# Gate layer norm moved to GpSimd, gated scaling to ScalarE, earlier reciprocals and two banks for the turned gate tiles

## The reference

```python
o_mla = mla_mixer(h_q, h_kv, k_pe, cos, sin, ...)   # 8 heads, full softmax over 512 keys
# spatial gating branch
z = gelu(h_sg); u, v = z[..., :512], z[..., 512:]
v = layernorm(v, ln_g, ln_b)                        # over the 512 channels of each token
mixed = einsum('hij,bcjhd->bcihd', w_s, v) + b_s    # inside chunks of 128 tokens
o_sg = u * mixed
o = concat([rmsnorm(o_mla, g1), rmsnorm(o_sg, g2)]) # then x = x + o @ w_out
```

## Time and profile before

| | us |
|---|---|
| median of 3 runs | 1542.7 (1542.68 to 1542.95) |
| profiled execution | 1543.31, its span 1541.5 |
| PE busy | 1464.7 (95% of the span) |
| DVE busy | 774.7 (50%) |
| ACT busy | 686.9 (45%) |
| POOL busy | 660.2 (43%) |

### The profile page before, as it was taken

The page is one execution under the profiler, slowest core; times in us unless marked ns, Lnnn a source line. Parts: engine busy times, 40 slices in busy tenths (PEclk is TensorE's granted clock), DMA queues, the critical chain, the costliest instruction groups (busy, mean ns, idle before and its releaser), DMA issues.

```text
span 1541.5 us, 19395 instructions
## 1 busy us (share of the span) xinstructions
PE 1464.7 (95%) x6838; PEld 1194.5 (77%) x6838; DVE 774.7 (50%) x1188; ACT 686.9 (45%) x1084; POOL 660.2 (43%) x317
## 2 busy tenths in 40 slices
PE   4998889999999999999999898999999999999994
PEld 4776669888878888888878565898888888888883
DVE  5738768633454530345164876792526445024443
ACT  4566636444343431344355664563534444124441
POOL 4443226743344444343545321585343444434440
PEclk9999999999999999999999999999999999999997
DMA  5320114521233243322423101354122332323221
GB/s 171 121 84 15 41 55 137 178 82 42 82 96 98 81 122 96 93 82 86 126 83 107 44 28 55 96 175 127 38 86 68 110 101 80 119 82 109 84 67 55
DMA packets 39032, 138.74 MB, mean 90 GB/s; under 512 B 4848, under 2 KB 5104, under 8 KB 38704
## 3 DMA queue, kind: packets, MB, share of 16 engines
q1 hardware_dynamic: 37440, 134.23, 28.4%
q10 hardware_dynamic: 1520, 3.52, 0.7%
HBM read 135.64 MB, written 2.10 MB: 89 GB/s over the span
## 4 chain that ended last, share of the span: by engine, by line
PE 78%; issue 10%; DVE 7%; POOL 4%; ACT 1%; POOLq 0%; DVEq 0%; ACTq 0%
PE ps L1284 25%; PE ps L1286 25%; PE ps L1285 25%; POOL w_lo L340 4%; PE ps L1436 1%; DVE small L988 1%; DVE h_lo L1014 1%; PE ps L1294 1%; DVE work L1091 0%; DVE small L1018 0%; DVE arena L1014 0%; PE ps L1459 0%; DVE work L1000 0%; DVE work L1074 0%; DVE arena L1164 0%
## 5 line engine op out<-in xcount | busy, mean ns | idle before, releaser
L340 POOL TENSOR_TENSOR w_lo<-raw,w_hi 128x1024 fp32r<-128x1024 f32 x248 | 605.0, 2457 | 721.0 <-ACT w_hi L436 720.8
L1284 PE MATMUL ps<-h_hi,w_hi 128*128 128x512 f32 (+1 forms) x1040 | 407.9, 392 | 26.0 <-POOL w_lo L340 20.5
L1285 PE MATMUL ps<-h_lo,w_hi 128*128 128x512 f32 (+1 forms) x1040 | 403.9, 388 | 0.0
L1286 PE MATMUL ps<-h_hi,w_lo 128*128 128x512 f32 (+1 forms) x1040 | 403.9, 388 | 0.0
L436 ACT ACTIVATE w_hi<-raw 128x1024 fp32r<-128x1024 f32 x248 | 255.8, 1054 | 326.6 <-PE ps L1286 326.5
L1284 PEld LDWEIGHTS ps<-h_hi,w_hi 128*128 128x128 f32 x1040 | 195.9, 188 | 69.3 <-issue 28.8
L1284 PE MATMUL ps<-arena,w_hi 128*128 128x512 f32 (+2 forms) x656 | 244.1, 372 | 0.9 <-DVE arena L970 0.9
L1286 PE MATMUL ps<-arena,w_lo 128*128 128x512 f32 (+2 forms) x656 | 241.9, 369 | 0.0
L1285 PE MATMUL ps<-arena,w_hi 128*128 128x512 f32 (+2 forms) x656 | 241.8, 369 | 0.0
L1285 PEld LDWEIGHTS ps<-h_lo,w_hi 128*128 128x128 f32 x1040 | 195.9, 188 | 40.8 <-issue 1.0
L1286 PEld LDWEIGHTS ps<-h_hi,w_lo 128*128 128x128 f32 x1040 | 195.8, 188 | 40.2
(11 more groups left out here) (169 smaller groups left out, 1793.5 us busy)
## 6 DMA issues: line engine op xcount, KB each, us to landing
raw<-blocks_d SPq DMA_DIRECT2D x248, 512.0 KB, 3.5
x<-xT_d SPq DMA_DIRECT2D x4, 512.0 KB, 7.7
work<-memT_d ACTq DMA_DIRECT2D x2, 1024.0 KB, 4.9
outT_d<-work SPq DMA_DIRECT2D x8, 256.0 KB, 2.2
work<-ln_d ACTq DMA_DIRECT2D x2, 512.0 KB, 3.6
par<-par_d ACTq DMA_DIRECT2D x2, 113.5 KB, 2.8
work<-pos_d ACTq DMA_DIRECT2D x1, 128.0 KB, 6.4
mix_g<-par_d ACTq DMA_DIRECT2D x2, 4.0 KB, 6.3
```

The source lines that it names most:

```text
L340: gp.tensor_tensor(w_lo[:, b % SPLIT, :], raw[:, b % RAW, :], w_hi[:, b % SPLIT, :].bitcast(F32), ALU.subtract).then_inc(lo_done.sem, 1)
L1284: pe.matmul(out, a_hi, b_hi, start=first, stop=False)
L1285: pe.matmul(out, a_hi, b_lo, start=False, stop=False)
L1286: return pe.matmul(out, a_lo, b_hi, start=False, stop=last)
```

## The change

- `recip_sums(h)` on DVE moves from the end of step (h, 3) to the end of (h, 2). All four exponentials of the head are then issued already, since ACT runs two steps ahead.
- The layer norm of the gate leaves DVE. DVE computes the roots at (1,1) and signals `gate_root`; POOL runs the three instructions per tile, tiles 0 and 1 at h 1, 2 and 3 at h 2, waiting for its own last instruction inside a tile. The `gate_low` calls follow them. ACT's hi parts move by one step each: SPLIT_STEPS from (1,2), (2,0), (2,2), (3,2) to (2,0), (2,1), (2,3), (3,1).
- The scaling of `u` leaves DVE for ACT, at the same steps, waiting for the new signal `gated_root`.
- `turn_gated(f)` uses banks 4 and 2 by turns, so that f 1 waits for nothing of its kind and f waits for the lo part of f-2. The output projection, whose first bank is 4, now waits for the lo part of f 2.

```diff
-NORM_STEPS = ((1, 1), (1, 3), (2, 1), (3, 1))
-SPLIT_STEPS = ((1, 2), (2, 0), (2, 2), (3, 2))
+ROOT_STEP = (1, 1)
+SPLIT_STEPS = ((2, 0), (2, 1), (2, 3), (3, 1))
...
+        BT = (4, 2)
...
+                def gate_norm(g):
+
+                    if g == 0:
+                        need(gate_root, 1)
+                        need(ln_in, 16)
+                    gp.tensor_scalar(vt[:, g, :], vt[:, g, :], mv[:, g, 0:1], sm_t[:, g:g + 1],
+                                     ALU.subtract, ALU.mult).then_inc(gate_step.sem, 1)
+                    need(gate_step, 2 * g + 1)
+                    gp.tensor_tensor(vt[:, g, :], vt[:, g, :], ln_gb[:, 0, :], ALU.mult).then_inc(gate_step.sem, 1)
+                    need(gate_step, 2 * g + 2)
+                    gp.tensor_tensor(vt[:, g, :], vt[:, g, :], ln_gb[:, 1, :], ALU.add).then_inc(vn_done.sem, 1)
...
-                        if h in (2, 3):
-                            gate_low(2 * h - 4)
-                            gate_low(2 * h - 3)
+                    if h == 1:
+                        gate_norm(0)
+                        gate_norm(1)
+                    if h == 2:
+                        gate_norm(2)
+                        gate_low(0)
+                        gate_norm(3)
+                        gate_low(1)
+                    if h == 3:
+                        gate_low(2)
+                        gate_low(3)
...
+                    if (h, t) in SCALED_STEPS:
+                        for c in ((0,), (1, 2), (3,))[SCALED_STEPS.index((h, t))]:
+                            need(gated_root, 1)
+                            act.activation(u[:, c, :], u[:, c, :], ACT.Copy, scale=sm_t[:, c:c + 1])\
+                                .then_inc(sg_normed.sem, 1)
...
-                    if (h, t) in NORM_STEPS:
-                        g = NORM_STEPS.index((h, t))
-                        if g == 0:
-                            need(ln_in, 16)
-                        link(dve.tensor_scalar(vt[:, g, :], vt[:, g, :], mv[:, g, 0:1], sm_t[:, g:g + 1],
-                                               ALU.subtract, ALU.mult))
-                        link(dve.tensor_tensor(vt[:, g, :], vt[:, g, :], ln_gb[:, 0, :], ALU.mult))
-                        dve.tensor_tensor(vt[:, g, :], vt[:, g, :], ln_gb[:, 1, :], ALU.add).then_inc(vn_done.sem, 1)
...
-                    if (h, t) in SCALED_STEPS:
-                        for c in ((0,), (1, 2), (3,))[SCALED_STEPS.index((h, t))]:
-                            dve.tensor_scalar(u[:, c, :], u[:, c, :], sm_t[:, c:c + 1], None, ALU.mult)\
-                                .then_inc(sg_normed.sem, 1)
+                        dve.sem_inc(gated_root.sem, 1)
...
-                    if t == 3:
+                    if t == 2:
                         recip_sums(h)
...
-                    else:
-                        need(sgl_done, f)
+                    elif f >= 2:
+                        need(sgl_done, f - 1)
...
-                        last = pe.transpose(ps[2][:, P * t:P * t + P], u[:, t, P * f:P * f + P], ident[:, :])
+                        last = pe.transpose(ps[BT[f % 2]][:, P * t:P * t + P], u[:, t, P * f:P * f + P], ident[:, :])
...
-                        bank_free=lambda j: need(o_done, HEADS) if j == 3 else None,
+                        bank_free=lambda j: need(*{0: (sgl_done, 3), 3: (o_done, HEADS)}[j]) if j in (0, 3) else None,
```

More of the change, by code:

```diff
@@ L225, in encoder_program @@
         vg_done = sig("vg_done", 4)
+        gate_root = sig("gate_root", 1)
+        gate_step = sig("gate_step", 2 * TT)
+        gated_root = sig("gated_root", 1)
         vn_done = sig("vn_done", 4)
@@ L285, in encoder_program @@
         pe_passed = ctx.enter_context(nc.semaphore("pe_passed"))
-        N_STEP = 77
+        N_STEP = 69
         dve_step = sig("dve_step", N_STEP)
@@ L574, in gate_turned @@
                     need(sg_turned, f + 1)
-                    act.activation(h_hi[:, 4 + f, :], ps[2][:, :], ACT.Copy,
+                    act.activation(h_hi[:, 4 + f, :], ps[BT[f % 2]][:, :], ACT.Copy,
                                    scale=par[:, G_SG + f:G_SG + f + 1]).then_inc(sgh_done.sem, 1)
@@ L1036, in gate_turned @@
                     need(sgh_done, f + 1)
-                    dve.scalar_tensor_tensor(out=h_lo[:, 4 + f, :], in0=ps[2][:, :],
+                    dve.scalar_tensor_tensor(out=h_lo[:, 4 + f, :], in0=ps[BT[f % 2]][:, :],
                                              scalar=par[:, G_SG + f:G_SG + f + 1], in1=h_hi[:, 4 + f, :].bitcast(F32),
@@ L1065, in layer @@
                             dve.tensor_scalar(sm_v, mv[:, :, 1], EPS, None, ALU.add).then_inc(s_v.sem, 1)
-                    if (h, t) == NORM_STEPS[0]:
+                    if (h, t) == ROOT_STEP:
                         small_root(1)
-                    if (h, t) in NORM_STEPS:
-                        g = NORM_STEPS.index((h, t))
-                        if g == 0:
-                            need(ln_in, 16)
-                        link(dve.tensor_scalar(vt[:, g, :], vt[:, g, :], mv[:, g, 0:1], sm_t[:, g:g + 1],
-                                               ALU.subtract, ALU.mult))
-                        link(dve.tensor_tensor(vt[:, g, :], vt[:, g, :], ln_gb[:, 0, :], ALU.mult))
-                        dve.tensor_tensor(vt[:, g, :], vt[:, g, :], ln_gb[:, 1, :], ALU.add).then_inc(vn_done.sem, 1)
+                        dve.sem_inc(gate_root.sem, 1)
                     if (h, t) in MIX_STEPS:
@@ L1081, in layer @@
                             need(gated, SG_HEADS)
+                            need(vn_done, 4)
                         statistics(u, GATED_STEPS.index((h, t)))
```

## The result

The changed kernel takes 1545.0 us (median of 17 runs, 1544.2 to 1545.8), the kernel before 1541.0 (17 runs, 1539.6 to 1543.9): ratio 1.0022, 95% interval 1.0015 to 1.0029. I had forecast 1535.0, within 1530.5 to 1541.5: outside the range, and wrong in sign. The profiled execution took 1545.4 us, its span 1543.2. That of before (1543.3) lies near the top of its runs, so the two traces differ by 1.7 us of span where the medians differ by 4.0. Of these 4.0 us 0.4 lie outside the span: every execution of the changed kernel takes 2.2 us beyond its span, every one of before 1.8.

A forecast was written before the change was run, and what follows sets the result against it. PE, busy 95% of the span, bounds the kernel; only its idle time can be won. 2 x (2.1 + 1.8) + 0.4 - 0.5 = 7.7 us off 1543.3 gives 1535.6, as median 1535.0, range 1530.5 to 1541.5.

The forecast's parts named there:

- What bounds: Both layers' stretches to the output projection: PE's idle time, about 16 us per layer, 33 in all, is the ceiling.
- PE's arrival at `mix(0)`: First half: with DVE relieved, PE would reach `mix(0)` 3.1 us sooner, at 893.2.
- POOL's norm per tile: Ahead of `mix(0)`: 3.9 us per tile, from 3.5 to 5.7, with 0.9 for the tensor_scalar.
- the forecast's gain of 2.1: First half: `mix(0)` starts at 895.7 and not 897.85, 2.1 us sooner per layer, bound by POOL.
- The clock: 0.4 us back for the shrinking gap at 175, 0.25 per layer charged for the longer gap ahead of `attend(7)`.
- Second half, sum: Steps up to the last attend: `attend(7)` starts 1.8 us sooner per layer.
- Second half, who brings it: Up to `attend(7)`: reciprocals one step sooner worth 0.1 us; the scaling moved to ACT credited with the 1.8.
- Banks: Turned gate tiles: two banks remove PE's waits of 1.79 and its like but win nothing of their own.
- POOL too slow: Rival at `mix(0)`: slower kernel from a tile norm of 5.1 us on, 1553 at 5.7; chance 0.11.
- The clock's rival: Clock falls in the 2.5 us gap ahead of `mix(0)` or stays low longer in the tail: 1538 to 1541; chance 0.15.

The follow-up runs named there:

- e12: e11 plus 4 + 2 more matmuls that nobody reads, in the waits for the exponentials at steps 27 and 28: 1525.0 us, ratio 0.9893 to the kernel before.
- e3: The changed kernel with the first instruction of each tile's norm on ScalarE, the two tensor_tensor left on GpSimd: 1530.4 us, ratio 0.9924 to the kernel before.
- e5: The changed kernel with GpSimd's tensor_scalar in four forms, one per tile, for durations only (tiles 1 to 3 get other values): one execution, 1541.2 us.
- e10: The kernel before with the two banks for the turned gate tiles alone: 1541.9 us, ratio 0.9998.
- e1: The kernel before with only the gate's layer norm on GpSimd and ScalarE's hi parts one step later: 1547.4 us, ratio 1.0042.
- e2: The changed kernel with the layer norm back on VectorE and SPLIT_STEPS as before: 1535.7 us, ratio 0.9964 to the kernel before.
- e6: The kernel before with the reciprocals alone one step sooner: 1534.5 us, ratio 0.9958.
- e9: The kernel before with the scalings of u alone moved to ScalarE, at the same steps: 1538.5 us, ratio 0.9977.
- e8: e3 with ten matmuls that nobody reads in the wait ahead of the last attend: 1527.3 us, ratio 0.9905 to the kernel before.
- e11: e3 with the scalings of u on GpSimd, and 3 + 10 unread matmuls ahead of the third turned gate tile and last attend: 1524.6 us, ratio 0.9889.

## Why the prediction was wrong, point by point

- **What bounds.** Right in the main: what the edits won lies in the gaps of the earlier trace rows, and every microsecond at the last `attend` counted. PE's idle time was not the ceiling, though. The lower clock lies in its busy time: 0.96 and 0.98 granted over the stretches of before, 1.00 in e12, whose fillers won it back.
- **PE's arrival at `mix(0)`.** Forecast 893.2 - 851.55 = 41.7 us behind the first turned scores; the changed kernel reached it at 42.4 (47.0 less the wait of 4.6) and e3, where nobody waits, at 42.06. Before it was 44.8, so 2.4 us were won and not 3.1: nearly right.
- **POOL's norm per tile: the step that failed.** 3.9 us forecast, 4.81 measured. The tensor_tensor (1.28) was right, the own wait is 0.08 and not 0.23, and the tensor_scalar is 2.08 where I took 0.9 and bounded it by 1.75. The reason that I gave, one tile read instead of two, is what e5 refutes. The nearest row by kind of work was the tensor_tensor and not a memset; its 1.28 as a floor would have given 4.3 and a gain of 1.1. With 4.81 put into the same sum, `mix(0)` is 1.0 us late; measured 0.7. That is 2.8 us per layer off the forecast's gain of 2.1. The mechanism and the queue's order were right, the term was wrong.
- **The clock: the second step that failed.** The sum charged nothing for a low clock behind `mix(0)`: a wait of 2.5 us there was to be harmless, against gaps of 1.70 and 1.50 that had not lowered the clock. The gap at 175 that I named as of that size is 1.66 us, and there the clock did fall, so size alone told nothing. With the wait at 4.6 us it fell, in both layers, and cost 2.1 and 2.75 (B). What 2.5 us would have done there no run shows. Against the kernel before this is the larger part: the late `mix(0)` costs 0.7 per layer, and C gives 1.4 to 2.0 back. The two failed steps together are 2 x 2.8 + 2.1 + 2.75 = 10.5 us, and the forecast missed by 10.0.
- **Second half, sum.** Forecast 1.8, measured 1.4 in the second layer (C; the 2.0 of the first contains a low stretch of before, at 175). The cause was right and ScalarE's scaling is 0.36 longer than I took for four: they follow one another at 0.61 us and not at 0.52.
- **Second half, who brings it.** I gave the reciprocals 0.1 and the scaling 1.8. Each alone brings 1.4 to 1.5 in C, and they do not add. I followed PE's wait for the reciprocal to `turned_lo` and stopped; I priced the scaling at its long durations of the earlier trace rows but didn't ask what made them long, and so not that a small shift could make them short.
- **Banks.** Nothing forecast, nothing measured. The output projection's new wait is hidden: D is unchanged within 0.15 in e10.
- **Rivals.** The slow one was the first, POOL too slow, at 0.11. It was put from 5.1 us per tile on and is real from 4.8, since the clock's fall comes with it. The clock's rival at 0.15 is the other half of the same event. I priced them as if independent. In the traces the waits of 4.4 to 4.6 us ahead of `mix(0)` (changed kernel, e1, e5) were followed by the lower clock in all six layers, those of 1.5 (before, e2, e6, e9, e10) in none of ten.

## What to carry to other kernels

An instruction form that the trace of before does not contain should be bounded by the dearest thing like it, with room above (2.08 lay beyond the 1.75 that I allowed), and where an engine is to become the feeder of a wait, the sum should be run once with that bound. Idle time of TensorE has a second price: if a gap lowers the clock, the work behind it is slower for microseconds, so two changes that each open a little wait may cost more than their waits, and the test is to fill the wait with matmuls that nobody reads. Of two edits that gain in the same place, measure each alone before adding them up: here one line alone gained 8 us, part of it by the place where the low clock fell, and with the rest of the change added the kernel was 4 us slower than before.

## What the runs showed of the hardware

- GpSimd, 128x512 f32 in SBUF: tensor_tensor 1.29 us; with one operand a spread column 1.04; tensor_scalar 1.50 with one operation, 1.93 with two, 2.08 with both operands from memory. The Trainium skill, GPSIMD Engine Reference, section Engine selection, holds one input to be roughly line rate; here the tensor_scalar, which reads one tile, is slower than the two input instruction, and the measurement decides.
- GpSimd, two instructions of which the second waits for the first: 0.08 us between them (POOL's rows of the changed kernel).
- VectorE's tensor_scalar on 128x512 f32 in SBUF takes 0.47 us with GpSimd idle and up to 2.14 beside a subtraction of GpSimd. The Trainium skill, GPSIMD Engine Reference, section Key points, names such contention for VectorE's two-port modes and for two SBUF inputs. That the instruction is longer beside GpSimd's the rows of e6 and of before show; in which mode it runs they don't.
- The lower clock level came in lengths of about 3.4 us or twice that, after different waits in different runs of like kernels: at 920 and at 934 in e3, at 179 in e8, at 917 in e11. Behind the same wait of 4.6 us it lasted 6.8 us in the changed kernel (both layers) and in e1's first layer, and 3.4 us in e1's second. Which of the short waits it follows, and what sets the length, these runs don't settle.
